# One 128x128 product per level for both token blocks, with the second block held reversed

## What is computed

```python
proj = h @ w_in                      # q, k (1024 each), v, r (2048 each), g_lr (16)
log_a = log_sigmoid(g_lr @ w_g2 + b_g2) / 16
# per head, with b the running sum of log_a inside a chunk:
diff = b_i[:, :, :, None, :] - b_i[:, :, None, :, :]
decay = exp(where(causal, diff, -inf))
attn = einsum('bhtk,bhsk,bhtsk->bhts', q_i, k_i, decay)
o = attn @ v_i + (q_i * exp(b_i)) @ state
...
o = rms_norm(o, o_gain);  return (o * silu(r)) @ w_o
```

## Time and profile before

| | |
|---|---|
| median of 3 timed runs | 2346.37 us (2344.70 to 2346.69) |
| profiled execution | 2346.09 us |
| its span in the profile | 2344.3 us |
| TensorE busy | 2334.3 us |
| VectorE, ScalarE, GpSimd busy | 1485.6, 1068.8, 140.8 us |
| HBM read | 432.38 MB, 185 GB/s over the span |

### The profile page before, as it was taken

How to read it: one execution, slowest core, us unless ns; L and a number is a source line. 1 busy time by engine, 2 the same in 40 slices (tenths; PEclk the granted TensorE clock), 3 DMA queues, 4 the chain that set the end, 5 groups by cost and what they waited for, 6 DMA issues and landing times.

```text
span 2344.3 us, 30085 instructions
## 1 busy us (share of the span) xinstructions
PE 2334.3 (100%) x10630; PEld 1936.5 (83%) x10630; DVE 1485.6 (63%) x1768; ACT 1068.8 (46%) x1240; POOL 140.8 (6%) x184
## 2 busy tenths in 40 slices
PE   9999999999999999999999999999999999999999
PEld 7788878888888888888888888888888888888887
DVE  5888558666666666666566555568666666665443
ACT  5544454444444444444444455445444444444333
POOL 2034110000000000000111110001000000000000
PEclk9999999999999999999999999999999999999999
DMA  6555545666666666555565565556666666666664
GB/s 210 160 182 149 157 150 187 202 196 190 194 192 194 192 194 193 193 194 192 177 197 175 161 215 165 158 173 195 197 191 195 194 191 196 189 194 201 203 201 143
DMA packets 229432, 435.62 MB, mean 186 GB/s; under 512 B 17524, under 2 KB 19672, under 8 KB 229224
## 3 DMA queue, kind: packets, MB, share of 16 engines
q1 hardware_dynamic: 224416, 430.49, 60.5%
q0 software_dynamic: 608, 3.69, 0.4%
q10 hardware_dynamic: 4328, 0.37, 0.1%
HBM read 432.38 MB, written 2.11 MB: 185 GB/s over the span
## 4 chain that ended last, share of the span: by engine, by line
PE 96%; DVE 1%; DMA 1%; ACT 1%; issue 0%; POOL 0%; ACTq 0%; SPq 0%; POOLq 0%; DVEq 0%
PE acc L345 31%; PE acc L347 31%; PE acc L346 31%; PE wk L466 1%; DMA raw<-in_fox_w_in_dram 1%; DVE w_lo L948 1%; PE tp L312 1%; PE wk L517 0%; ACT w_hi L581 0%; ACT act L619 0%; PE tp L527 0%; DVE gla_kT L1124 0%; PE wk L441 0%; PE tp L401 0%; PE wk L545 0%
## 5 line engine op out<-in xcount | busy, mean ns | idle before, releaser
L948 DVE TENSOR_TENSOR w_lo<-raw,w_hi 128x1024 fp32r<-128x1024 f32 x816 | 1016.3, 1256 | 683.7 <-ACT w_hi L581 682.2
L581 ACT ACTIVATE w_hi<-raw 128x1024 fp32r<-128x1024 f32 x816 | 858.9, 1059 | 1006.4 <-PE acc L347 961.3
L345 PE MATMUL acc<-w_hi,xt_hi 128*128 128x512 f32 x2304 | 903.8, 392 | 4.7 <-DVE w_lo L948 4.6
L347 PE MATMUL acc<-w_hi,xt_lo 128*128 128x512 f32 x2304 | 897.1, 389 | 0.0
L346 PE MATMUL acc<-w_lo,xt_hi 128*128 128x512 f32 x2304 | 896.6, 389 | 0.0
L345 PEld LDWEIGHTS acc<-w_hi,xt_hi 128*128 128x128 f32 x2304 | 432.6, 188 | 98.7 <-DVE w_lo L948 5.5
L347 PEld LDWEIGHTS acc<-w_hi,xt_lo 128*128 128x128 f32 x2304 | 432.5, 188 | 90.2
L346 PEld LDWEIGHTS acc<-w_lo,xt_hi 128*128 128x128 f32 x2304 | 432.7, 188 | 89.3 <-issue 1.0
L346 PE MATMUL acc<-w_lo,ht_hi 128*128 128x512 f32 x704 | 273.9, 389 | 0.0
L345 PE MATMUL acc<-w_hi,ht_hi 128*128 128x512 f32 x704 | 273.9, 389 | 0.0
L347 PE MATMUL acc<-w_hi,ht_lo 128*128 128x512 f32 x704 | 273.9, 389 | 0.0
(11 more groups left out here) (181 smaller groups left out, 898.9 us busy)
## 6 DMA issues: line engine op xcount, KB each, us to landing
raw<-in_ffn_w_gate_dram SPq DMA_DIRECT2D x176, 512.0 KB, 4.4
raw<-in_ffn_w_up_dram SPq DMA_DIRECT2D x176, 512.0 KB, 4.3
raw<-in_ffn_w_down_dram SPq DMA_DIRECT2D x176, 512.0 KB, 4.5
raw<-in_fox_w_in_dram SPq DMA_DIRECT2D x128, 512.0 KB, 5.3
raw<-in_gla_w_in_dram SPq DMA_DIRECT2D x96, 512.0 KB, 4.0
raw<-in_gla_w_o_dram SPq DMA_DIRECT2D x32, 512.0 KB, 4.2
raw<-in_fox_w_o_dram SPq DMA_DIRECT2D x32, 512.0 KB, 3.8
xres<-in_x_dram SPq DMA_DIRECT2D x8, 256.0 KB, 6.6
```

What stands on the lines that cost most here:

```text
L345: pe.matmul(o, xh, wh, start=(k == 0), stop=False)
L347: last = pe.matmul(o, xl, wh, start=False, stop=(k == chunks * KC_CHUNK - 1))
L581: nc.scalar.activation(w_hi[:, slot, :], raw[:, slot, :], ACT.Copy).then_inc(hi_done, 1)
L948: nc.vector.tensor_tensor(w_lo[:, slot, :], raw[:, slot, :], w_hi[:, slot, :].bitcast(F32), ALU.subtract).then_inc(lo_done, 1)
```

## The change

The second token block is held reversed. A new matrix `flip`, the identity with its columns in reverse, takes the place of `ident` where block 1 is turned on TensorE (x at the start, y at the end of the mixer), and one small product with it turns the norm's factors (`flip_rstd`, `gla_rstd`). In a reversed block the keys of a pair of halves stand where in block 0 the queries stand. `factors` therefore puts the key side of both blocks into the first 128 columns of fac and the query side of both into the second, and `level_product` makes one product of 128x128 for both blocks: block 0's weights lie on one side of the diagonal, block 1's on the other. They are gathered in a new tile `ac`, and `part_weights` splits it at the end. Block 1's running sum becomes a sum over the tokens before, and `running_sums` writes the difference to the last token into dec. The reordering: squares among the first tile's splits, the narrow split behind the last `hi` and `lo`, the wait for the norm moved from before tile 1's splits to where tile 0 is emptied, and `gate_rest` from slot (3, 1) to (3, 2).

```diff
@@ tensor
             def turn(n, second=ident):
...
                         last = pe.transpose(tp[:, kk, b * P:(b + 1) * P], stage[:, b, kk * P:(kk + 1) * P],
-                                            ident[:, :])
+                                            (second if b else ident)[:, :])
...
+            def flip_rstd():
+                pe.wait_ge(rstd_ready, 1)
+                pe.matmul(wk[:, 1, 0:TB], flip[:, :], rstd[:, 0, :], start=True, stop=True).then_inc(rstd_flipped, 1)
...
-                for b in range(1 if kind == "far" else TB):
+                for b in range(TB if kind == "diag" else 1):
...
-                            elif kind == "far":
+                            else:
                                 ks, qs = f[:, ft, 0:P], f[:, ft, P:S]
-                            else:
-                                ks = qs = f[:, ft, b * P:(b + 1) * P]
...
                 if t == 0:
                     narrow_product(wn_hi, wn_lo, 0)
+                    flip_rstd()
@@ scalar
+            def gla_rstd():
+                ac.wait_ge(rstd_ready, 1)
+                ac.wait_ge(rstd_flipped, 1)
+                nc.scalar.activation(grstd[:, 0:1], rstd[:, 0, 0:1], ACT.Copy)
+                nc.scalar.activation(grstd[:, 1:2], wk[:, 1, 1:2], ACT.Copy).then_inc(grstd_ready, 1)
...
+                nc.scalar.activation(qrstd[:, :], grstd[:, :], ACT.Copy, scale=(KD // GH) ** -0.5) \
+                    .then_inc(grstd_ready, 1)
+                ac.wait_ge(grstd_ready, 2)
...
-                if m == 1:
-                    nc.scalar.activation(dec[:, :, P:S], bT[:, :, P:S], ACT.Exp, scale=1.0 / 16)
-                    nc.scalar.activation(dec[:, :, 0:P], dec[:, :, 0:P], ACT.Exp,
-                                         scale=1.0 / 16).then_inc(dec_done, 1)
-                else:
-                    nc.scalar.activation(dec[:, :, :], dec[:, :, :], ACT.Exp, scale=1.0 / 16).then_inc(dec_done, 1)
+                nc.scalar.activation(dec[:, :, :], dec[:, :, :], ACT.Exp, scale=1.0 / 16).then_inc(dec_done, 1)
...
             def empty(t):
+                if t == 0:
+                    gla_rstd()
...
                     for j in range(CH):
                         half_x(j)
+                        hi(c0, j)
+                        small_loads(j)
                         if j == CH - 1:
                             narrow_split(wn, wn_hi, 0)
-                        hi(c0, j)
-                        small_loads(j)
-                    for n in range(DT):
-                        squares(None, 0, n)
+                        if j % 2:
+                            squares(None, 0, j // 2)
                 else:
-                    if t == 1:
-                        ac.wait_ge(rstd_ready, 1)
-                        link(nc.scalar.activation(qrstd[:, :], rstd[:, 0, :], ACT.Copy, scale=(KD // GH) ** -0.5))
@@ vector
             def running_sums():
...
+                nc.vector.tensor_tensor(gtot[:, :, 0:1], minz[:, :, S - 1:S], dec[:, :, S - 1:S], ALU.subtract)
+                nc.vector.memset(bT[:, :, P:P + 1], 0.0)
                 for f in range(GF):
-                    for b in range(TB):
-                        s = slice(b * P, (b + 1) * P)
-                        last = nc.vector.tensor_tensor_scan(bT[:, f, s], minz[:, f, s], dec[:, f, s], 0.0,
-                                                            ALU.add, ALU.subtract)
-                last.then_inc(b_done, 1)
+                    nc.vector.tensor_tensor_scan(bT[:, f, 0:P], minz[:, f, 0:P], dec[:, f, 0:P], 0.0,
+                                                 ALU.add, ALU.subtract)
+                    last = nc.vector.tensor_tensor_scan(bT[:, f, P + 1:S], minz[:, f, P:S - 1], dec[:, f, P:S - 1], 0.0,
+                                                        ALU.add, ALU.subtract)
+                link(last)
+                link(nc.vector.tensor_tensor(gtot[:, :, 1:2], gtot[:, :, 0:1], bT[:, :, S - 1:S], ALU.add))
+                nc.vector.tensor_tensor(dec[:, :, P:S], gtot[:, :, 1:2].to_broadcast([P, GF, P]), bT[:, :, P:S],
+                                        ALU.subtract).then_inc(b_done, 1)
...
+                def part(t, b, upper):
+                    return t[:, :, b * P:(b + 1) * P].rearrange("p f (g two h) -> p f g two h", two=2,
+                                                                h=LEVELS[m - 2])[:, :, :, upper, :]
+                for side, src, b, upper in ((0, kT, 0, 0), (0, kT, 1, 1), (1, qT, 0, 1), (1, qT, 1, 0)):
+                    last = nc.vector.tensor_tensor(part(f, side, upper), part(src, b, upper), part(dec, b, upper),
+                                                   ALU.mult)
+                last.then_inc(fac_done, 1)
...
+                    elif m == 2:
+                        last = nc.vector.tensor_copy(ac[:, :, :], src)
+                    else:
+                        last = nc.vector.copy_predicated(ac[:, :, :], every_head(m - 3), src)
...
+            def part_weights():
+                ve.wait_ge(a_kept, len(levels) + 1)
+                nc.vector.copy_predicated(a0[:, :, 0:P], every_head(len(LEVELS) - 1), ac[:, :, :])
+                nc.vector.copy_predicated(a1[:, :, :], every_head(len(LEVELS)), ac[:, :, :]).then_inc(a_kept, 1)
...
-                    (2, 2): gate_u, (3, 1): gate_rest}
+                    (2, 2): gate_u, (3, 2): gate_rest}
...
                     for j in range(CH):
                         half_x(j)
-                        if j == CH - 1:
-                            narrow_split(wn, wn_hi, wn_lo, 0)
                         lo(c0, j)
+                    narrow_split(wn, wn_hi, wn_lo, 0)
@@ gpsimd
             for m, h in enumerate(LEVELS):
                 po.wait_ge(fac_done, m + 1)
-                b4 = bT[:, :, :].rearrange("p f (g two h) -> p (f g) two h", two=2, h=h)
-                d4 = dec[:, :, :].rearrange("p f (g two h) -> p (f g) two h", two=2, h=h)
-                ref = b4[:, :, 0, h - 1:h].to_broadcast([P, GF * S // (2 * h), h])
-                nc.gpsimd.tensor_tensor(d4[:, :, 0, :], ref, b4[:, :, 0, :], ALU.subtract)
-                nc.gpsimd.tensor_tensor(d4[:, :, 1, :], b4[:, :, 1, :], ref, ALU.subtract).then_inc(d_done, 1)
+                for b in range(TB):
+                    b4 = bT[:, :, b * P:(b + 1) * P].rearrange("p f (g two h) -> p f g two h", two=2, h=h)
+                    d4 = dec[:, :, b * P:(b + 1) * P].rearrange("p f (g two h) -> p f g two h", two=2, h=h)
+                    ref = b4[:, :, :, 0, h - 1:h] if b == 0 else b4[:, :, :, 1, 0:1]
+                    ref = ref.to_broadcast([P, GF, P // (2 * h), h])
+                    nc.gpsimd.tensor_tensor(d4[:, :, :, 0, :], ref, b4[:, :, :, 0, :], ALU.subtract)
+                    last = nc.gpsimd.tensor_tensor(d4[:, :, :, 1, :], b4[:, :, :, 1, :], ref, ALU.subtract)
+                last.then_inc(d_done, 1)
```

More of the change, by code:

```diff
@@ L304, in _, with turn @@
         def _(pe):
-            def turn(n):
+            def turn(n, second=ident):
                 wait(pe, tp_hi, n)
@@ L327, in tile @@
                         if turn_n is not None:
-                            turn(turn_n)
+                            turn(turn_n, second)
                         if mid is not None:
@@ L401, in half_turn @@
                         last = pe.transpose(tp[:, 2 * (h % 2) + kk, b * P:(b + 1) * P],
-                                            xres[:, b, k * P:(k + 1) * P], ident[:, :])
+                                            xres[:, b, k * P:(k + 1) * P], (flip if b else ident)[:, :])
                 last.then_inc(half_turned, 1)
@@ L487, in _ @@
             jobs[slots[first + 1]] = lambda: o_product(1)
-            jobs[slots[first + 2]] = lambda: (turn(Lin(gy)), o_product(2))
-            jobs[slots[first + 3]] = lambda: (turn(Lin(gy + 1)), o_product(3))
-            jobs[slots[first + 4]] = lambda: turn(Lin(gy + 2))
+            jobs[slots[first + 2]] = lambda: (turn(Lin(gy), flip), o_product(2))
+            jobs[slots[first + 3]] = lambda: (turn(Lin(gy + 1), flip), o_product(3))
+            jobs[slots[first + 4]] = lambda: turn(Lin(gy + 2), flip)
             for t in range(2 * QT + 2 * DT):
@@ L646, in turn_y, with scaled @@
                 last.then_inc(tp_hi, 1)
-            def scaled(dst, pair, used, norm, func, done, free=None):
+            def scaled(dst, pair, used, scale, func, done, free=None):
                 wait(ac, chunk_used, used)
@@ L855, in stage_raw @@
             def stage_raw(t):
-                scaled(lambda b: stage[:, b, :], t.base % 2, Lin(cf + (t.base + 1) * CH, t.per * CH, t.reg), 2,
-                       ACT.Copy, raw_qk, free=t + gq)
+                scaled(lambda b: stage[:, b, :], t.base % 2, Lin(cf + (t.base + 1) * CH, t.per * CH, t.reg),
+                       rstd[:, 2, :], ACT.Copy, raw_qk, free=t + gq)
             def fox_turn(t):
@@ L1230, in _ @@
             for m in range(1, len(levels) + 1):
```

(5 more changed lines are left out.)

95 lines of the change are left out of this document (56 added, 39 removed).

## The result

Over four runs of each kernel the changed one takes 2330.43 us (median; 2330.30 to 2331.13) and the one before 2345.61 us (2344.70 to 2346.69): ratio 0.9935, 95% interval 0.9924 to 0.9947: 0.65% faster, well clear of no change. The profiled execution of the changed kernel took 2331.13 us, with a span of 2329.4 us.

What follows compares the result with a forecast made beforehand. TensorE's instruction stream plus its gaps was taken as the bound. From the profiled 2346.09 us, -12.5 - 1.05 - 1.4 + 1.4 = -13.55 gave 2332.5 us; the 8-in-10 range was 2331.0 to 2337.0.

Steps and rivals of the forecast that it cites:

- The level products: TensorE's products in seven levels halve from 3.57 to 1.78 us each: -12.5 us, half tile 12.69 us.
- The chain of a level: GpSimd differences, exponential, factors and hand-overs of a level take 12.56 us against a 12.69 us slot: cost 0.
- P: Turn of one half-size GpSimd difference in a level, taken as 0.93 us; cost nothing below 0.96.
- rival (a): Level chain mildly becomes the bound, P 1.0 to 1.25: 2333.6 to 2339.5 us, most likely 2335; chance 0.22.
- running_sums, longer: Added VectorE operations before chunk 3's split in tile 5 make a new TensorE stall: +1.4 us, bounds 0.9 and 1.9.
- cover for factors(1): After running_sums, factors(1) and its split come 1.6 us later, TensorE 1.4 later; 0.48 us of slack holds.
- The start: Reordered work in tile 0 shrinks one gap by 0.4 and closes another, new flip matmul costs 0.25: -1.05 us.
- gate_rest, one slot later: Moving this VectorE work in tile 3 to its next slot, in tile 4, removes a TensorE wait: -1.4 us.
- (b): Rival: half-size GpSimd differences cost nearly a whole one, P 1.75, level chain 3.2 us over: 2351.5 us; chance 0.08.
- (c): Rival: no new stall at running_sums, since the added operations overlap the scans: 2331.1 us; chance 0.06.
- (d): Rival: the start backfires, squares do not fit or tile 0 is emptied late: 2333.5 us; chance 0.04.
- (e): Rival: the halved level products free nothing on TensorE: 2344.8 us; chance 0.01.

Runs made afterwards that it cites:

- e5: The changed kernel with the last sum and subtract of running_sums behind chunk 3's split in tile 5, GpSimd released only after the subtract; 2330.09 us, ratio 0.9931.
- e3: The changed kernel with squares, narrow split and gate_rest back in their old places; 2333.19 us, ratio 0.9947 to the kernel before.
- e7: The changed kernel with the squares alone back behind all eight hi splits of tile 0; 2331.03 us in one execution.
- e1: The kernel before, run again without edit; 2346.58 us, median of 11, ratio 1.0001.
- e8: The changed kernel, run again without edit; 2331.00 us, ratio 0.9935 to the kernel before.
- e4: The changed kernel with the last sum and subtract of running_sums behind chunk 3's split, GpSimd's difference starting straight after the scans; 2331.14 us, ratio 0.9937.
- e6: The changed kernel with each of GpSimd's four differences of a level cut in two; 2331.33 us, ratio 0.9938 to the kernel before.

## Why the prediction was right in kind and 2 us off

**The level products**, -12.5: measured -12.48, in 1.78 us and slots of 12.68. Right, and so was the reading that TensorE's stream sets the time.

**The chain of a level**, 0: right. GpSimd's part was forecast at 4.30 + 4P = 8.0 us and took 7.94 in the first level, so P is 0.91; over the levels it is 0.90 to 1.02. At 1.02, above the 0.96 where I let the cost begin, TensorE still doesn't wait, because my sum compared one level with one slot and had no term for a lead over several. The turns behind that sum are shown by the pieces of 0.61 and 1.60 us, with one correction: a turn is lost only to a VectorE operation that stands ready. The Trainium skill says that of a VectorE operation with two SBUF inputs and a GpSimd operation that reads SBUF, the one that starts first holds the shared port pair for its whole instruction (SBUF — State Buffer, "SBUF: two separate sides"). The pieces of 0.61 and 1.60 us agree with that. That the two then alternate is my reading of the rows, and the 6.19 us of the earlier trace rows go against it. The Trainium skill's rate of about 2.6 cycles an element (GPSIMD Engine Reference, "Elementwise — side-by-side cycle accounting"), rival (a)'s support, gives an estimate of 1.1 us for a half-size turn. The trace doesn't agree: it has 0.91.

**running_sums, longer**, +1.4: measured +1.40, before chunk 3, for w_lo, as forecast. That the sum fits to 0.01 is partly luck. The split comes 1.55 us later after the diagonal product than before (145.04 - 133.58 against 146.32 - 136.41), where I took 1.7, and TensorE's matmul 1.15 us later (146.31 - 133.58 against 147.99 - 136.41). The rest, 0.25, comes behind the wait, a part of it in longer matmuls, for which the forecast had no term. The move of both operations behind the split (e5) takes 1.34 of it back, which shows the cause. Its cover for factors(1) held.

**The start**, -1.05: measured -1.19. The new matmul costs 0.14 us, not 0.25. The first gap went from 0.60 to 0.22 as said. What I had only half seen is that the squares' place is a condition: the splits that now stand ahead of the norm slow GpSimd's small operations from 0.20 to 1.06 us, and with the squares late TensorE waits (e3, e7).

**gate_rest, one slot later**, -1.4: measured -1.87, mis-sized by 0.5. The kernels e3 and after differ in tiles 1 to 4 by its place alone, and by 1.84 us (94.16 and 92.32). I priced one stall of 1.36 us. The lateness of VectorE reached into the next tile. One row of TensorE of the kernel before, at the first chunk of tile 4:

```profile
114.35 0.50 PE L345 MATMUL acc<-w_hi,xt_hi 128*128 128x512 f32 x1
```

A matmul of 0.50 us instead of 0.39 follows an interrupted stream. I had both the earlier trace rows and this lengthened row at hand, and took the wait's bracket for the whole loss; the excess from start to start is 1.37 at the first and 0.19 at the second, and each resumption costs about 0.11 more (0.50 - 0.39) in the matmuls behind it: 1.37 + 0.19 + 0.22 = 1.78, of the 1.87.

**The step that failed** is the one in which I wrote "I sum against 2346.09". The earlier trace rows lists five waits for w_lo. I dealt with those at 32.66, 42.06 and 111.27 and never asked where the longest of the five, 1.3 us, stood, and so carried a wait in FoX at its full length into the forecast as if that length were part of the kernel. It is not: the same kernel ran that stretch in 91.74 us in the next trace, 1.16 less.

From the profiled 2346.09 to the profiled 2331.13 it is 14.96 us against my 13.55. Of these 1.41 us, 0.47 are gate_rest, the second thing mis-sized, -0.09 the start with its later first matmul, and 0.99 the untouched rest, 1.40 less in FoX's logits and 0.41 more elsewhere; 0.04 is what lies around the span and rounding. The remaining 0.7 us to the median of 2330.43 lie inside the spread of one kernel (2329.98 to 2331.56 in nine runs), for which my range had left 0.3, although the three known times of before already spanned 2.0. With 1.16 less in the base and gate_rest at 1.87 the sum would have been 2330.9, an estimate from these two corrections. The profiled time was close to the median of before, which made it look a safe base. The traces account only for the two profiled executions: by the medians the kernels are 15.2 us apart here and 15.1 in the second group (2346.06 and 2331.00), against the 14.14 of the stretches that the change touches. That 1 us of difference is about as much as a median of one kernel moves (e1), and whether it is chance or follows the change isn't shown.

**The rivals.** (a) and (b) fall by GpSimd's 7.90 to 8.38 us and by the missing waits in tiles 6 to 9, (c) by the wait in tile 5; that the time came out near its 2331.1 is no sign of it. (d) falls by a tile 0 that is 1.19 us shorter. (e) falls by the 12.48.

**What stays open.** Why FoX's weights land late in some executions isn't settled: ScalarE waited 3.82 us for such a transfer in e1, 4.90 before, 5.27 in e8 and 5.56 in the first trace of after, where TensorE lost only 0.38. No run changed the order of the loads. Why the wait stands at about 1380 with the old levels and at about 1156 with the new ones is open too. Nor is it known why the far product's difference on GpSimd took 6.19 us before, letting all four splits pass, and takes 2.80 in the kernel after, 2.88 in e4 and 2.80 in e5. Strict alternation explains the later values, not the first.

## What to carry to other kernels

Before a time is summed against a profiled execution, each wait in its table has to be named, and asked whether the kernel or that execution made it. A second trace of the same kernel shows which lengths repeat. The range has to be as wide as the spread of the times already known. A stall is sized from start to start, with the longer matmul at its end, and not by the bracket alone. Work cut into more pieces for an engine that alternates with another pays a turn for each operation that stands ready on the other side and no more; here the cut added no turn, only the cost of the extra pieces. A chain that is a little longer than its slot costs nothing until its lead is used up, so it is judged over all its rounds.

## What the runs showed of the hardware

- Most of GpSimd's operations on 128x2 elements take 0.20 us alone (before) and up to 1.06 while VectorE has splits queued (e3): a small operation can pay the other's whole turn, 1.08 us.
- A 128x256 difference takes 0.61 us alone and 1.60 with a split in its way (e6). A 128x1024 subtract of VectorE takes 1.23 alone (e5) and 2.81 beside one of GpSimd (e4).
- The product with flip, two records of two columns, holds TensorE for 0.14 us, and the first matmul after an interruption takes 0.47 to 0.50 us instead of 0.39.
- The mean granted clock of every profiled execution was 1.00, the upper level of 2.4 GHz, so none of the differences is the clock's.
